# Sums of squares of four norms as one 512-column product of a split operand, and the key column sums moved behind the kv projection, in a two-layer decoder trunk

## The chip, the cores and the metric

The kernel runs on one core of a Trainium2 chip. Its time is the device time of one execution in microseconds (us); before the change the median of three runs is 1017.04 us (1016.98 to 1017.77). One more execution was recorded by the hardware profiler. The engines are named as in its page: PE is the matrix engine, PEld its weight loads, DVE the vector engine, ACT the scalar engine, POOL GpSimd, SP the engine that issues the weight DMAs.

## What is computed

The input x is 256 tokens by 1024 numbers in float32. Two layers follow each other. Each is a macaron block: half a feed-forward, a mixer, half a feed-forward, each of them behind an RMS norm. The first mixer is a retention with 4 heads, the second a sliding-window attention with 16 query heads, whose keys and values are made once, from x as it stands after the first layer. Cut to what matters here:

```python
def rms_norm(x, g):
    y = x * rsqrt(mean(x * x, axis=-1) + 1e-6)
    return y * g

def swiglu(h, w_in, w_out):                    # 1024 -> 2 x 2816 -> 1024
    gate, up = split(h @ w_in, 2)
    return (silu(gate) * up) @ w_out

x = x + 0.5 * swiglu(rms_norm(x, g1), ...)     # feed-forward f = 0, norm m = 0
x = x + retention(rms_norm(x, gm))             #                     norm m = 1
x = x + 0.5 * swiglu(rms_norm(x, g2), ...)     # f = 1, m = 2
k, v = split(rms_norm(x, g_kv) @ w_kv, 2)      # the shared keys and values, of the same x as m = 3
k = rope(rms_norm(k))
x = x + 0.5 * swiglu(rms_norm(x, g1), ...)     # f = 2, m = 3
x = x + attention(rms_norm(x, gm), k, v)       #        m = 4
x = x + 0.5 * swiglu(rms_norm(x, g2), ...)     # f = 3, m = 5
```

## The kernel before

**Layout.** x lies transposed: 8 tiles of 128 features by 256 tokens. Each of the engines has its own program, written out by hand and tied to the others by semaphores (`wait_ge`, `then_inc`); nothing is scheduled by a tool. What stands first in an engine's program runs first, and a wait holds back all that stands behind it on that engine.

**Split products.** Every weight and every activation is held as two parts, high and low (`w_hi`, `w_lo`; `h` holds the high part of a tile in its first 256 columns and the low part in the next 256). A block of weights is used in a pair of products: `w_hi` with all 512 columns, then `w_lo` with the first 256. `weight_block` issues such pairs alternately; where `high_product` and `low_product` are called in loops, several high products come first and then as many low ones ("in passes").

**Weights.** They come in units of 2048 or 1408 columns through 4 slots. SP issues a unit's DMA once the slot is free, ACT makes `w_hi` (its `split`), DVE makes `w_lo = stage - w_hi` (its `split`, L648, counted by the semaphore `lo_ready`), and PE waits for `lo_ready` (or for `hi_ready` where it runs in passes).

**Norms.** The norm's factor is not applied to h but to the products. In a feed-forward's first groups of products (`in_group`, 8 blocks kt of 4 pairs each per group), PE also adds up the squares (`norm_sum`): a product of a 128 x 128 matrix of ones with `sq_sum`, both in plain float32, gives the sum in all rows of a PSUM bank. DVE reads it (`token_sums`, L668) and makes the inverse root (`token_scale`, nine small steps). For m = 2 and 3 `norm_sum` stands behind kt = 5 of group 0; for m = 0 and 5 behind kt = 4 of group 1. `sq_sum` is made on POOL tile by tile as x becomes ready (`square_sum`, L1122 to L1131), and for m = 0 on DVE (`first_sums`, L1073), in front of the split of weight unit 3.

**Key columns.** The keys are needed with tokens in rows, so their norm factor is needed as a column. For m = 3 `norm_sum` therefore also issues two products with 2 columns each (`ones` moving, `sq_sum` as weights), and DVE makes `r_col` from them in `token_scale` and counts `r_ready`. That is long before they are used.

**The end of feed-forward 2.** Its output tiles 0 to 5 are made in pairs (`out_tile`). Then PE runs the kv projection (`shared_kv`), and output tiles 6 and 7 in passes (`out_tile_in_passes`, L1295), whose weights are four units of their own (`last_out`). Meanwhile ACT waits for `r_ready`, copies keys and values out of PSUM with the factor, and DVE runs `shared_k` (L830), the norm and rotation of the keys; the DVE split of the last of the four units stands behind it, then the evacuation of tile 6 and two splits of the query weights, the evacuation of tile 7, one more split, and the rotation of the first queries (`q_rope`). PE then runs the query products and waits for that rotation before it transposes the queries (`q_transposes`, L1473).

## Time and profile before

| | |
|---|---|
| median of three runs | 1017.04 us (1016.98 to 1017.77) |
| the profiled execution | 1017.42 us, of which its span 1015.6 us |
| granted TensorE clock | 1.00 |
| PE busy | 1011.0 us, 100% |
| PE weight loads | 885.8 us, 87% |
| DVE busy | 780.5 us, 77% |
| ACT busy | 496.9 us, 49% |
| POOL busy | 95.9 us, 9% |

The span runs from the first to the last instruction; the 1.8 us around it belong to the execution as a whole. A busy PE is not a PE at its peak, since its instructions overlap: what one product costs is the distance from its start to the start of the next.

### The profile page before, as it was taken

How to read it: one execution, taken by the hardware profiler on the slowest of the kernel's cores; microseconds unless marked ns; L12 is line 12 of the kernel's file. 1: busy time of each engine (PE TensorE's matmuls, PEld its weight loads, DVE VectorE, ACT ScalarE, POOL GpSimd, SP SyncE). 2: the span in 40 equal slices, each digit the busy share in tenths (PEclk: the TensorE clock that was granted, in tenths of full speed). 3: DMA queues.
4: the chain of work that ended last, by engine and by line, in shares of the span. 5: the costliest groups of instructions: out<-in, count | busy, mean ns of one | idle time of the engine just before them, and what ended most of it. 6: DMA issues, size and time to landing. Idle time of an engine off the chain costs nothing.

```text
span 1015.6 us, 15838 instructions
## 1 busy us (share of the span) xinstructions
PE 1011.0 (100%) x5922; PEld 885.8 (87%) x5922; DVE 780.5 (77%) x874; ACT 496.9 (49%) x536; POOL 95.9 (9%) x91
## 2 busy tenths in 40 slices
PE   9999999999999999999999999999999999999998
PEld 8888888888888888888888888888897898888888
DVE  7988866787797787777767787787778977877743
ACT  7455435544443364454444454465447944554432
POOL 0000013101100151000013100000220041000000
PEclk9999999999999999999999999999999999999999
DMA  9664456652553454554455645545563345544461
GB/s 347 242 235 178 142 175 220 245 195 104 218 191 103 187 184 162 199 200 169 150 187 197 249 165 192 190 145 171 183 241 120 106 161 192 207 168 165 156 192 65
DMA packets 32295, 185.31 MB, mean 182 GB/s; under 512 B 3840, under 2 KB 6400, under 8 KB 16128
## 3 DMA queue, kind: packets, MB, share of 16 engines
q1 hardware_dynamic: 31968, 184.64, 50.8%
q8 instruction: 23, 0.38, 0.1%
q14 instruction: 16, 0.13, 0.1%
q10 hardware_dynamic: 288, 0.16, 0.1%
HBM read 183.73 MB, written 1.05 MB: 182 GB/s over the span
## 4 chain that ended last, share of the span: by engine, by line
PE 100%; issue 0%; DVE 0%; DVEq 0%
PE ps L1159 99%; PE ps L1506 1%; PE ps L1473 0%; PE ps L1465 0%; DVE x L813 0%; DVE ones L1086 0%; DVEq L1085 0%; DVEq L1084 0%; DVEq L1083 0%; DVEq L1082 0%; DVEq L1081 0%
## 5 line engine op out<-in xcount | busy, mean ns | idle before, releaser
L1159 PE MATMUL ps<-h,w_hi 128*128 128x512 f32 x1664 | 563.3, 394 | 0.0
L1159 PE MATMUL ps<-h,w_lo 128*128 128x256 f32 x1664 | 437.8, 278 | 0.0
L648 DVE TENSOR_TENSOR w_lo<-stage,w_hi 128x2048 fp32r<-128x2048 f32 (+1 forms) x190 | 397.2, 2100 | 32.5 <-ACT w_hi L333 32.3
L1159 PEld LDWEIGHTS ps<-h,w_hi 128*128 128x128 f32 x1664 | 310.0, 188 | 68.5 <-issue 0.3
L333 ACT ACTIVATE w_hi<-stage 128x2048 fp32r<-128x2048 f32 (+1 forms) x190 | 326.9, 1728 | 6.4 <-PE ps L1159 6.2
L1159 PEld LDWEIGHTS ps<-h,w_lo 128*128 128x128 f32 x1664 | 304.8, 188 | 3.3
L1159 PE MATMUL ps<-act_t,w_hi 128*128 128x512 f32 (+1 forms) x726 | 240.0, 386 | 0.0
L1159 PE MATMUL ps<-act_t,w_lo 128*128 128x256 f32 x704 | 189.3, 278 | 0.0
L1159 PEld LDWEIGHTS ps<-act_t,w_hi 128*128 128x128 f32 x726 | 134.4, 188 | 29.0
L365 ACT ACTIVATE tmp<-ps 128x1024 f32<-128x1024 f32 x44 | 45.1, 1025 | 193.4 <-PE ps L1159 193.4
L1159 PEld LDWEIGHTS ps<-act_t,w_lo 128*128 128x128 f32 x704 | 130.0, 188 | 0.3
L712 DVE TENSOR_TENSOR tmp<-ps,tmp 128x1024 f32<-128x1024 f32 x44 | 53.8, 1224 | 70.0 <-ACT tmp L365 70.0
L398 ACT ACTIVATE tmp<-ps 128x256 f32<-128x256 f32 x39 | 14.9, 381 | 119.1 <-PE ps L1159 119.1
L1159 PE MATMUL ps<-w_hi,h 128*128 128x512 f32 x192 | 60.3, 395 | 0.0
L758 DVE SCALAR_TENSOR_TENSOR tmp<-ps,tmp 128x256 f32<-128x256 f32 x39 | 16.5, 422 | 54.0 <-ACT tmp L398 54.0
L370 ACT ACTIVATE tmp<-tmp 128x512 f32<-128x512 f32 x44 | 27.9, 633 | 58.9 <-DVE tmp L718 58.9
L718 DVE TENSOR_TENSOR tmp<-tmp,r_row 128x1024 f32<-128x1024 f32 x44 | 53.9, 1225 | 1.5
L1131 POOL TENSOR_TENSOR sq_sum<-sq_sum,sq 128x256 f32<-128x256 f32 x35 | 48.5, 1384 | 2.8
L1122 POOL TENSOR_TENSOR sq_sum<-x 128x256 f32<-128x256 f32 x5 | 3.1, 614 | 442.8 <-DVE x L760 379.7
L1128 POOL TENSOR_TENSOR sq<-x 128x256 f32 x35 | 31.0, 885 | 130.6 <-DVE x L760 128.6
L1159 PEld LDWEIGHTS ps<-w_hi,h 128*128 128x128 f32 x192 | 35.1, 188 | 7.8 <-issue 0.7
L687 DVE SCALAR_TENSOR_TENSOR h<-x,gain,h 128x256 fp32r<-128x256 f32 (+1 forms) x48 | 32.7, 682 | 10.2 <-ACT h L344 10.1
(158 smaller groups left out, 711.0 us busy)
## 6 DMA issues: line engine op xcount, KB each, us to landing
stage<-w_in_dram SPq DMA_DIRECT2D x85, 1024.0 KB, 4.8
stage<-w_out_dram SPq DMA_DIRECT2D x64, 704.0 KB, 4.0
stage<-w_ret_dram SPq DMA_DIRECT2D x24, 1024.0 KB, 4.9
stage<-w_ret_out_dram SPq DMA_DIRECT2D x8, 1024.0 KB, 4.8
stage<-w_q_dram SPq DMA_DIRECT2D x4, 1024.0 KB, 6.2
stage<-w_o_dram SPq DMA_DIRECT2D x4, 1024.0 KB, 4.8
stage<-w_in_dram SPq DMA_DIRECT2D x8, 256.0 KB, 4.3
stage<-w_in_dram SPq DMA_DIRECT2D x2, 512.0 KB, 6.3
```

The source lines that it names most:

```text
L333: nc.scalar.activation(w_hi[:, s, 0:n], stage[:, s, 0:n], ACT.Copy).then_inc(hi_ready, 1)
L365: nc.scalar.activation(t, ps[:, 4 * (g % 2):4 * (g % 2) + 4, T:2 * T], ACT.Copy).then_inc(in_lo_half, 1)
L370: nc.scalar.activation(tmp[:, g % 2, 0:512], tmp[:, g % 2, 0:512], ACT.Silu).then_inc(in_silu, 1)
L398: nc.scalar.activation(tmp[:, d % 2, 0:T], ps[:, bank, T:2 * T], ACT.Copy, scale=scale).then_inc(out_lo_half, 1)
L648: nc.vector.tensor_tensor(w_lo[:, s, 0:n], stage[:, s, 0:n], w_hi[:, s, 0:n].bitcast(F32), ALU.subtract).then_inc(lo_ready, 1)
L687: nc.vector.scalar_tensor_tensor(h[:, ds(d + per * i, 1), T:2 * T], x[:, ds(d + per * i, 1), :], gain[:, ds(m * DT + d + per * i, 1)], h[: ...
L712: nc.vector.tensor_tensor(t, ps[:, 4 * (g % 2):4 * (g % 2) + 4, 0:T], t, ALU.add).then_inc(in_free, 1)
L718: nc.vector.tensor_tensor(t, t, same(r_row[:], 4), ALU.mult).then_inc(in_scaled, 1)
L758: chain.step(nc.vector.scalar_tensor_tensor(t, ps[:, bank, 0:T], scale, t, ALU.mult, ALU.add))
L1128: nc.gpsimd.tensor_tensor(sq[:].rearrange("p (a n) -> p a n", a=1), x[:, ds(i + 1, 1), :], x[:, ds(i + 1, 1), :], ALU.mult).then_inc(sq_do ...
L1131: nc.gpsimd.tensor_tensor(sq_sum[:], sq_sum[:], sq[:], ALU.add).then_inc(sum_added, 1)
L1159: return nc.tensor.matmul(out_, w, x_, start=start, stop=stop)
```

## The change

Three things change. For the four norms ahead of feed-forwards (m = 0, 2, 3, 5) the sum of squares is itself split into a high and a low part, side by side in `sq_parts`, and `norm_sum` is one product of 512 columns in the type of the split weights; DVE adds the two halves with a second instruction. The block of four pairs in front of that product is issued alternately instead of in passes. And the two key column products move from `norm_sum` (m = 3) to behind the kv projection, with the DVE steps for `r_col` in front of `shared_k`; tiles 6 and 7 of feed-forward 2 are made with `out_tile`, so alternately.

```diff
                 dve.wait_ge(sum_done, sums_before(m) + 1)
-                ins = nc.vector.tensor_scalar(n_v[:], ps[:, FIRST_SUM if m in LATE_NORMS else SUM, 0:T], V_SCALE / D, V_SCALE * EPS,
-                                              ALU.mult, ALU.add)
-                if m == 3:
-                    ins = nc.vector.tensor_scalar(col_v[:], ps[:, SUM, T:T + 4], V_SCALE / D, V_SCALE * EPS, ALU.mult, ALU.add)
+                bank = FIRST_SUM if m in LATE_NORMS else SUM
+                ins = nc.vector.tensor_scalar(n_v[:], ps[:, bank, 0:T], V_SCALE / D, V_SCALE * EPS, ALU.mult, ALU.add)
+                if m in FFN_NORM:
+                    ins.then_inc(half_added, 1)
+                    dve.wait_ge(half_added, FFN_NORM.index(m) + 1)
+                    ins = nc.vector.scalar_tensor_tensor(n_v[:], ps[:, bank, T:2 * T], V_SCALE / D, n_v[:], ALU.mult,
+                                                         ALU.add)
                 ins.then_inc(sum_read, 1)
...
                 rsqrt(n_v[:], n_t[:], r_row[:])
-                if m == 3:
-                    rsqrt(col_v[:], col_t[:], r_col[:])
-                    nc.vector.tensor_copy(col_t[:], r_col[:]).then_inc(r_ready, 1)
+
+            def key_columns():
+
+                dve.wait_ge(columns_done, 1)
+                chain.step(nc.vector.tensor_scalar(col_v[:], ps[:, COLUMNS, T:T + 4], V_SCALE / D, V_SCALE * EPS,
+                                                   ALU.mult, ALU.add))
+                rsqrt(col_v[:], col_t[:], r_col[:])
+                nc.vector.tensor_copy(col_t[:], r_col[:]).then_inc(r_ready, 1)
...
                     out_evac(m, 5, (u + 14, u + 15), 0.5)
+                    key_columns()
                     shared_k()
                     split(FIRST["kv", 0] + 4)
...
-                nc.vector.tensor_tensor(sq_sum[:], x_sq[:, 0, :], x_sq[:, 1, :], ALU.add).then_inc(sum_added, DT)
+                nc.vector.tensor_tensor(sq_all[:], x_sq[:, 0, :], x_sq[:, 1, :], ALU.add).then_inc(sum_added, DT)
+                dve.wait_ge(sum_added, DT)
+                nc.vector.tensor_scalar(sq_parts[:, 0:T], sq_all[:], 1.0, None, ALU.mult).then_inc(sq_hi, 1)
+                dve.wait_ge(sq_hi, 1)
+                nc.vector.tensor_tensor(sq_parts[:, T:2 * T], sq_all[:], sq_parts[:, 0:T].bitcast(F32),
+                                        ALU.subtract).then_inc(sq_lo, 1)
...
+                if parts:
+                    pool.wait_ge(sum_added, added_for(m) - 1)
+                    pool.wait_ge(x_done, CREDIT + DT * m)
+                    nc.gpsimd.tensor_tensor(sq[:], x[:, DT - 1, :], x[:, DT - 1, :], ALU.mult).then_inc(sq_done, 1)
+                    pool.wait_ge(sq_done, (DT - 1) * m)
+                    nc.gpsimd.tensor_tensor(sq_all[:], sq_sum[:], sq[:], ALU.add).then_inc(sum_added, 1)
+                    n = FFN_NORM.index(m)
+                    pool.wait_ge(sum_added, added_for(m))
+                    nc.gpsimd.tensor_copy(sq_parts[:, 0:T], sq_all[:]).then_inc(sq_hi, 1)
+                    pool.wait_ge(sq_hi, n + 1)
+                    nc.gpsimd.tensor_tensor(sq_parts[:, T:2 * T], sq_all[:], sq_parts[:, 0:T].bitcast(F32),
+                                            ALU.subtract).then_inc(sq_lo, 1)
...
                 pe.wait_ge(sum_added, added_for(m))
-                if m in (3, ATT):
-                    for t in range(2):
-                        last = matmul(ps[:, SUM, T + 2 * t:T + 2 * t + 2], sq_sum[:, t * P:(t + 1) * P],
-                                      ones[:, 0:2], True, True)
-                if m != ATT:
-                    last = matmul(ps[:, FIRST_SUM if m in LATE_NORMS else SUM, 0:T], ones[:], sq_sum[:], True, True)
+                if m == ATT:
+                    last = column_sums(SUM, sq_sum)
+                elif m in FFN_NORM:
+                    pe.wait_ge(sq_lo, FFN_NORM.index(m) + 1)
+                    last = matmul(ps[:, FIRST_SUM if m in LATE_NORMS else SUM, :], ones[:].bitcast(F32R), sq_parts[:],
+                                  True, True)
+                else:
+                    last = matmul(ps[:, SUM, 0:T], ones[:], sq_sum[:], True, True)
                 last.then_inc(sum_done, 1)
...
-                        ahead_of_sum = g == 0 or (g == 1 and kt <= 4) if m in LATE_NORMS else m == 2 and kt <= 5
+                        ahead_of_sum = g == 0 or (g == 1 and kt <= 3) if m in LATE_NORMS else m == 2 and kt <= 4
...
                 if f == 2:
                     shared_kv()
+                    column_sums(COLUMNS, sq_all).then_inc(columns_done, 1)
                     for d in range(2):
-                        out_tile_in_passes(f, d, pairs)
+                        out_tile(f, d, pairs)
```

Where instructions move, the programs of the engines show it. The first place is DVE's program at the very start, where the squares of the input are added up ahead of the split of weight unit 3. Before:

```order
L1077 TENSOR_TENSOR x_sq<-x_sq 128x1024
L1078 TENSOR_TENSOR x_sq<-x_sq 128x512
L1079 TENSOR_TENSOR sq_sum<-x_sq 128x256
L648 TENSOR_TENSOR w_lo<-stage,w_hi 128x2048
L712 TENSOR_TENSOR tmp<-ps,tmp 128x1024
```

The same place in the changed kernel:

```order
L1090 TENSOR_TENSOR x_sq<-x_sq 128x1024
L1091 TENSOR_TENSOR x_sq<-x_sq 128x512
L1092 TENSOR_TENSOR sq_all<-x_sq 128x256
L1094 TENSOR_SCALAR sq_parts<-sq_all 128x256
L1096 TENSOR_TENSOR sq_parts<-sq_all,sq_parts 128x256
L652 TENSOR_TENSOR w_lo<-stage,w_hi 128x2048
L724 TENSOR_TENSOR tmp<-ps,tmp 128x1024
```

Two instructions of 256 columns now stand in front of the split.

The second place is DVE's program behind the kv projection; `w_lo` of 1408 columns is the split of the third `last_out` unit, `k_a` begins `shared_k`. Before:

```order
L687 SCALAR_TENSOR_TENSOR h<-x,gain,h 128x256
L648 TENSOR_TENSOR w_lo<-stage,w_hi 128x1408
L836 TENSOR_TENSOR k_a<-kv_nat 128x256
L837 TENSOR_REDUCE hs_110<-k_a 128x4
L838 TENSOR_SCALAR hs_111<-hs_110 128x4
```

The same place in the changed kernel:

```order
L690 TENSOR_SCALAR col_v<-ps 128x4
L657 TENSOR_SCALAR r_col<-col_v 128x4
L663 TENSOR_TENSOR col_t<-r_col 128x4
L664 TENSOR_TENSOR col_t<-col_t,col_v 128x4
L665 SCALAR_TENSOR_TENSOR col_t<-col_t 128x4
L666 SCALAR_TENSOR_TENSOR r_col<-col_t,r_col 128x4
L661 SCALAR_TENSOR_TENSOR col_t<-r_col 128x4
L664 TENSOR_TENSOR col_t<-col_t,col_v 128x4
L665 SCALAR_TENSOR_TENSOR col_t<-col_t 128x4
L666 SCALAR_TENSOR_TENSOR r_col<-col_t,r_col 128x4
L693 COPY col_t<-r_col 128x4
L849 TENSOR_TENSOR k_a<-kv_nat 128x256
```

Eleven small instructions of 4 columns each, which stood behind the inverse root of m = 3, now stand between the split and `shared_k`.

The third place is POOL's program at the end of each `square_sum` ahead of a feed-forward. Before, the loop is followed by the next use of the routine:

```order
L1128 TENSOR_TENSOR sq<-x 128x256
L1130 REGISTER_ALU
L1131 TENSOR_TENSOR sq_sum<-sq_sum,sq 128x256
L1123 REGISTER_ALU
L1123 COMPARE_AND_BRANCH
L1122 TENSOR_TENSOR sq_sum<-x 128x256
```

In the changed kernel:

```order
L1150 TENSOR_TENSOR sq_sum<-sq_sum,sq 128x256
L1142 REGISTER_ALU
L1142 COMPARE_AND_BRANCH
L1154 TENSOR_TENSOR sq<-x 128x256
L1156 TENSOR_TENSOR sq_all<-sq_sum,sq 128x256
L1159 CAST sq_parts<-sq_all 128x256
L1161 TENSOR_TENSOR sq_parts<-sq_all,sq_parts 128x256
L1140 TENSOR_TENSOR sq_sum<-x 128x256
```

The last tile's square and addition are written out, and a copy and a subtraction follow them.

## Rows read from the trace of the kernel before

**Rows 1.** Page, part 1: busy time, share of the span and instructions of each engine

```profile
PE 1011.0 (100%) x5922; PEld 885.8 (87%) x5922; DVE 780.5 (77%) x874; ACT 496.9 (49%) x536; POOL 95.9 (9%) x91
```

**Rows 2.** Timeline of PE around the sum of m = 0: start, duration, engine, instruction

```profile
23.13 1.09 PE L1159 MATMUL ps<-h,w_hi 128*128 128x512 f32 x4
24.06 0.64 PE L1159 MATMUL ps<-h,w_lo 128*128 128x256 f32 x4
24.54 0.60 PE L1159 MATMUL ps<-sq_sum,ones 128*128 128x256 f32 x2
...
25.31 0.40 PE L1159 MATMUL ps<-h,w_hi 128*128 128x512 f32 x1
...
40.22 0.39 PE L1159 MATMUL ps<-h,w_hi 128*128 128x512 f32 x1
```

**Rows 3.** Timeline of PE around the sum and the key columns of m = 3

```profile
577.35 0.50 PE L1159 MATMUL ps<-ones,sq_sum 128*128 128x2 f32 x4
...
578.58 0.39 PE L1159 MATMUL ps<-h,w_hi 128*128 128x512 f32 x1
```

**Rows 4.** Timeline of DVE, then of the weight loads, in the first 30 us

```profile
20.25 0.43 DVE L1079 TENSOR_TENSOR sq_sum<-x_sq 128x256 f32<-128x256 f32 x1
20.59 2.28 DVE L648 TENSOR_TENSOR w_lo<-stage,w_hi 128x2048 fp32r<-128x2048 f32 x1
...
28.66 0.29 DVE L653 TENSOR_SCALAR r_row<-n_v 128x256 int32<-128x256 int32 x1
...
23.02 0.77 PEld L1159 LDWEIGHTS ps<-h,w_hi 128*128 128x128 f32 x4
```

**Rows 5.** Timeline of DVE: first and last of the ten steps of `r_col`

```profile
582.96 0.17 DVE L653 TENSOR_SCALAR r_col<-col_v 128x4 int32<-128x4 int32 x1
...
584.74 0.17 DVE L681 COPY col_t<-r_col 128x4 f32<-128x4 f32 x1
```

**Rows 6.** Timeline of ACT, then of DVE, from the kv projection to the queries

```profile
743.65 0.62 ACT L440 ACTIVATE kv_nat<-ps,r_col 128x128 f32<-128x128 f32 x2 [2.43 <-PE ps L1159]
...
744.31 0.42 DVE L836 TENSOR_TENSOR k_a<-kv_nat 128x256 f32<-128x256 f32 x1 [0.40 <-ACT kv_nat L440]
...
750.12 1.62 DVE L648 TENSOR_TENSOR w_lo<-stage,w_hi 128x1408 fp32r<-128x1408 f32 x1
...
755.00 4.49 DVE L648 TENSOR_TENSOR w_lo<-stage,w_hi 128x2048 fp32r<-128x2048 f32 x2 [1.29 <-ACT w_hi L333]
...
766.35 0.69 DVE L825 TENSOR_TENSOR q_a<-q_a,q_b 128x512 f32<-128x512 f32 x1
...
777.81 0.69 DVE L825 TENSOR_TENSOR q_a<-q_a,q_b 128x512 f32<-128x512 f32 x1
```

**Rows 7.** Timeline of PE, then of the weight loads, from the kv projection on

```profile
743.45 2.68 PE L1159 MATMUL ps<-act_t,w_hi 128*128 128x512 f32 x11
...
758.78 0.60 PE L1465 MATMUL ps<-ident,k_twice 128*128 128x128 f32 x4
...
767.66 0.60 PE L1473 MATMUL ps<-ident,q_a 128*128 128x128 f32 x4
...
778.62 0.42 PEld L1473 LDWEIGHTS ps<-ident,q_a 128*128 128x128 f32 x4 [0.21 <-issue]
```

**Rows 8.** Timelines of DVE, POOL and the weight loads, end of the retention

```profile
364.09 2.29 DVE L648 TENSOR_TENSOR w_lo<-stage,w_hi 128x2048 fp32r<-128x2048 f32 x1 [0.79 <-ACT w_hi L333]
...
364.19 2.79 POOL L1131 TENSOR_TENSOR sq_sum<-sq_sum,sq 128x256 f32<-128x256 f32 x1
...
389.06 0.61 POOL L1128 TENSOR_TENSOR sq<-x 128x256 f32 x1 [3.97 <-DVE x L760]
389.75 0.81 POOL L1131 TENSOR_TENSOR sq_sum<-sq_sum,sq 128x256 f32<-128x256 f32 x1
...
391.25 2.29 DVE L648 TENSOR_TENSOR w_lo<-stage,w_hi 128x2048 fp32r<-128x2048 f32 x1 [1.29 <-ACT w_hi L333]
...
393.76 0.31 PEld L1159 LDWEIGHTS ps<-sq_sum,ones 128*128 128x128 f32 x2
```

More of the change, by code:

```diff
@@ L195, in trunk @@
     ps = nc.alloc_psum_tensor("ps", [P, 8, 512], F32)
-    SUM, FIRST_SUM = 7, 3
+    SUM, FIRST_SUM, COLUMNS = 7, 3, 3
     sem = nc.alloc_semaphore
@@ L1122, in square_sum @@
                 nc.gpsimd.tensor_tensor(sq_sum[:], x[:, 0, :], x[:, 0, :], ALU.mult).then_inc(sum_added, 1)
-                with pool.Fori(0, DT - 1) as i:
+                parts = m in FFN_NORM
+                with pool.Fori(0, DT - 2 if parts else DT - 1) as i:
                     pool.wait_ge(sum_added, added_for(m) - DT + 1 + i)
@@ L1293, in ffn @@
                     out_tile(f, 1, pairs, whole_block)
[L1295 to L1308 removed]
             def out_tile(f, d, i, block=weight_block):
                 m, u0 = FFN_NORM[f], FIRST["out", f]
+                if f == 2 and isinstance(i, int):
+                    u0 = FIRST["last_out", f] - 4 * i
                 pe.wait_ge(x_done, DT * m + d + 1 + 2 * i)
```

22 lines of the change are left out of this document (9 added, 13 removed).

## The prediction, made before the changed kernel ran

> **What bounds the kernel now.** I read the page's busy times first: PE is busy 1011.0 of 1015.6 us [rows 1], DVE 780.5. So nearly every microsecond that PE's stream gets longer or shorter is one of the total, and work on DVE, ACT or POOL costs nothing until PE waits for it. Then I read PE's timeline around each place that the change touches, by the distances between starts, and last, for each of these places, how long before PE's need the other engines are done. The reader is to see in those rows what a sum costs PE, and how little air there is at two places.
>
> **PE's own work, removed and added.** A pair of products in alternation takes 0.347 us (14.91 us from 25.31 to 40.22 for 43 pairs), in passes 0.353 (23.13 to 24.54, four pairs) [rows 2]. The float32 sum of 256 columns starts at 24.54 and the second pair behind it at 25.31: 0.77 for one pair and the sum, so the sum costs 0.42. The new sum is one product of 512 columns of the split type. Four such, the high ones of a pass, start 0.93 apart in all, 0.23 each [rows 2]; I take 0.23, so 0.19 is saved at each of m = 0, 2 and 5, together 0.57. Should the new product cost as much as the old, that is nothing; it can't cost less than 0.23, since no wide product in the rows does.
>
> At m = 3 the key columns and the sum together take 577.35 to 578.58, 1.23 less one pair of 0.35, so 0.88 [rows 3]. With the new sum 0.23 stays, and 0.65 goes. Of that 0.88 less 0.42, so 0.46, are the key columns, which come back behind the kv projection. The blocks in front of the three other sums gain 0.006 a pair, 0.02 each, 0.07 for all three with rounding. PE's stream therefore loses 0.57 + 0.65 + 0.07 = 1.29 us before the kv projection, and there it gains 0.46 and loses at most 44 x 0.006 = 0.26 by the alternation of tiles 6 and 7 (0.1 if a long pass costs less per pair than a short one). What counts there is decided by a wait, below.
>
> **The start: two steps ahead of a split that was just in time.** DVE's split of unit 3 runs 20.59 to 22.87, and PE starts to load weights from it at 23.02 [rows 4]. That is 0.15 us of air, and a semaphore from DVE to PE takes about 0.12 (the rotation ends at 778.50 [rows 6], PE's load starts at 778.62 [rows 7]), so 0.03 is left. The change puts two dependent steps in between: a copy of 256 columns, 0.29 as the one-input step of the same size, and a subtraction, 0.43 as the addition ahead of it [rows 4], with some 0.03 of gap before each. The split moves by 0.78 and PE waits 0.75 (0.6 to 0.9 with other gaps; nothing only if the two steps ran beside the split, which one engine can't do). Behind PE's wait stands its whole program, and nothing later in the first feed-forward hands it back. I take 0.75.
>
> **Behind the kv projection: the key columns go from covered to exposed.** Before, ACT takes the keys out of PSUM at 743.65, as soon as PE is done, because `r_ready` was counted long ago; DVE's `k_a` follows at 744.31 [rows 6]. Now PE first issues the columns: they would start where tile 6 did, at 743.45 [rows 7], and are done 0.50 later [rows 3], 743.95. DVE reads them (0.2 with the gap) and does the ten steps from 582.96 to 584.91, 1.95 us [rows 5]: `r_ready` comes at about 746.13, ACT's copies start at 746.17 in place of 743.65, and everything behind them on DVE is 2.5 us late.
>
> Who waits for that? First the split of the fourth `last_out` unit: it ended at 751.74 [rows 6], now 754.26. PE needs it after three half tiles, 743.45 + 0.46 + 3 x 3.83 = 755.4 (a half tile is a quarter of 743.45 to 758.78 [rows 7]): 1.1 us of air, so the switch from `hi_ready` to `lo_ready` is free. Next the two splits of the query weights: they start at 755.00 and follow on tile 6's evacuation through ACT, so they start at 757.5, the first ends near 759.8, and PE wants it at about 759.5: a wait of 0.4. Then tile 7's evacuation, one more split, and the rotation of the first queries, whose last step ended at 767.04 [rows 6] with PE's transposes at 767.66 [rows 7]: it now ends at 769.6, and PE waits there again. On the way DVE was busy or waited for ACT, and ACT waited for DVE's x; these 1.29 us idles [rows 6] are part of the chain and absorb nothing. At last the second rotation, 778.50 then, 781.0 now; there PE's load engine already sat idle 0.21 us before the change [rows 7], so no air is left at all and PE is late by the full 2.5. From there both engines go on 2.5 us later. This is not beside the 0.46 and the 0.1 to 0.26 above but contains them: PE reaches the waits 0.4 later or 0.1 earlier and stands there until DVE is done. I take 2.5; the ends are 0.2 (all of DVE's lateness absorbed, only the columns left: 0.46 less 0.26) and 3.5 (the small steps at 0.3 in place of 0.2 us each).
>
> **POOL's two more steps.** At m = 2 POOL's last addition ends at 390.56 and PE loads the sum's weights at 393.76 [rows 8]. A copy and a subtraction come in between. The subtraction is an addition of 0.81. The trace shows no copy on POOL; its nearest row is the square of one tile, 0.61, an upper bound, and the lower is nothing. Taken alone they are done by 392.1, 1.6 us early. But DVE's split starts at 391.25, and the trace shows what that can do: the addition at 364.19 came 0.10 behind the start of a split (364.09 to 366.38) and took 2.79 in place of 0.81, so it ran only once the split was over [rows 8]. If the subtraction starts before 391.25 the split is the one to wait, and it has time. If it starts after, it ends at 393.54 + 0.7 = 394.2, PE's load goes to 394.3, and that costs 0.5. The copy must take less than about 0.5 us. A one-input step should be cheaper than one that reads two operands, so I take no collision: 0, with 0.5 as the other end.
> The Trainium skill, "SBUF — State Buffer", section "SBUF: two separate sides", calls the port pair that DVE and GpSimd share an exclusive lock: whoever starts first has it for the whole instruction, and the other is blocked. The row at 364.19 agrees, and by this rule the order of two starts some tenths apart decides over 0.5 us here. By "GPSIMD Engine Reference" of the Trainium skill, section "Elementwise — side-by-side cycle accounting", a loop body of at most two operations takes 1.03 cycles an element and a two-input step about 2.6, which at 1.2 GHz makes the copy an estimated 0.22 us plus dispatch; no row of before shows it, and by that figure the subtraction would win the race.
> At m = 3 and 5 the same two steps follow a tile that ends as far ahead of its sum or further, and I take them as hidden, collision or not. DVE's added instruction in `token_sums` (0.43, as the addition of rows 4) delays the root by half a microsecond, while PE has 8 pairs or more, 2.8 us, until it waits for the read; hidden.
>
> **The sum.** -1.29 + 0.75 + 2.5 = +1.96 us. It is made on the profiled execution, 1017.42 us (span 1015.6 and 1.8 around it), which gives 1019.4. That execution was 0.4 above the median, so for the median I say 1017.04 + 1.96 = 1019.0 us. What a measurement of this kernel can tell from no change is 0.2%, 2.03 us; the forecast lies on that line, 1019.07, just inside it.
>
> **Rivals.**
> - A, the race on the shared port is lost: as above plus 0.5, 1019.5. For it: POOL's steps have gaps of about 0.1 and the margin is 0.2 or less. Against: the copy reads one operand.
> - B, DVE catches up before the first transposes, so it is not slower: the place is the stretch from the kv projection to 767.66, the price falls from 2.5 to 0.2. It decides whether the rotation that ended at 767.04 moves by less than PE's 0.62 of air. Then -1.29 + 0.75 + 0.2 = -0.3: 1016.7, no change. Against: no idle of DVE there is free of its own chain.
> - C, as B, and the first split is not late for PE either: -1.29 + 0.2 = -1.1, 1015.9. It needs both waits to be absent; rows 4 speak against it.
> - D, the late chain grows: if the small steps take 0.3, or PE's restarts behind its waits each cost some tenths, the 2.5 becomes 3.5 and the whole 1020.0; with the race lost too, 1020.5.
> - E, the new sum is no cheaper than the old one (the low half, or the switch to it, eats the gain): 4 x 0.19 dearer, 1019.8.
>
> **Chances and range.** Forecast 0.42, A 0.18, B 0.15, C 0.06, D 0.12, E 0.07. A, D and E lie above 1019.07, 0.37 together, and 0.15 of the forecast's 0.42 does too: slower 0.52. No change has the other 0.27 of the forecast and B and C but for 0.03, so 0.45; faster has that 0.03. No case reaches 1015.0, where faster begins, without a gain that no row shows. The forecast's own range is 1018.5 to 1019.5. The range that should hold 8 in 10 takes in A, most of D and E, and most of B: 1016.6 to 1020.4.
>
> **What would show it.** In the changed profile: PE's distance from the 512-column sum's start to the next start near 0.23; PE idle about 0.75 us near 23, with the weight load behind it at 23.8 in place of 23.02; `kv_nat` 2.5 us after the kv projection's end; PE idle before the query products and before the first two transposes of queries, in all a span from the kv projection's end to the second transposes 2.5 us longer than the 35.2 of before. At the end of the retention, the copy on POOL under 0.5 us and the subtraction 0.8, not 2.8. The forecast is wrong if PE shows no wait at 23 us, if the first transposes follow at the old distance, or if the sum takes PE 0.4 us or more.

## The result, and the profile after

The changed kernel takes a median of 1022.17 us in 15 executions (1018.75 to 1022.47), the kernel before 1017.31 in 15 (1016.98 to 1017.83): a ratio of 1.0034 by the means (1.0048 by the medians), 95% interval 1.0027 to 1.0042. The prediction was 1019.0, its range 1016.6 to 1020.4. But the 15 times are not spread, they lie in two groups: 7 at 1018.75 to 1019.50 and 8 at 1022.17 to 1022.47, with nothing between them. The kernel before has one group. The granted clock is 1.00 in both groups (0.999 in single executions), so it is not the clock that parts them. The profiled execution is of the lower group (1019.50 us, span 1017.7), and there the prediction's steps can be read one by one.

The page of the kernel after (against [rows 1]):

```profile
span 1017.7 us, 15830 instructions
PE 1010.2 (99%) x5918; PEld 888.0 (87%) x5918; DVE 783.3 (77%) x880; ACT 497.0 (49%) x536; POOL 99.2 (10%) x97
```

PE is busy 0.8 us less than before in a span 2.1 us longer: in this execution PE waits more, it does not work more.

The start, from the timelines of DVE, the weight loads and PE (answering [rows 4] and [rows 2]; in brackets the idle time of the engine before the row and what ended it):

```profile
20.92 0.29 DVE L1094 TENSOR_SCALAR sq_parts<-sq_all 128x256 fp32r<-128x256 f32 x1
21.24 0.43 DVE L1096 TENSOR_TENSOR sq_parts<-sq_all,sq_parts 128x256 fp32r<-128x256 f32 x1
21.59 2.28 DVE L652 TENSOR_TENSOR w_lo<-stage,w_hi 128x2048 fp32r<-128x2048 f32 x1
...
23.92 0.19 PEld L1190 LDWEIGHTS ps<-h,w_hi 128*128 128x128 f32 x1 [1.49 <-DVE w_lo L652]
...
25.44 0.40 PE L1190 MATMUL ps<-sq_parts,ones 128*128 128x512 f32 x1
25.68 0.40 PE L1190 MATMUL ps<-h,w_hi 128*128 128x512 f32 x1
```

The two steps stand in front of the split, PE waits for it, and the new product costs 25.44 to 25.68, 0.24, as worked out. The sum starts 0.90 later than before (24.54 in [rows 2]).

The kv projection and what follows, from the timelines of PE, ACT, DVE and the weight loads (answering [rows 6, 7]):

```profile
743.29 0.50 PE L1190 MATMUL ps<-ones,sq_all 128*128 128x2 f32 x4
...
746.07 0.63 ACT L444 ACTIVATE kv_nat<-ps,r_col 128x128 f32<-128x128 f32 x2 [5.01 <-DVE col_t L693]
...
746.73 0.43 DVE L849 TENSOR_TENSOR k_a<-kv_nat 128x256 f32<-128x256 f32 x1 [0.75 <-ACT kv_nat L444]
...
759.68 0.30 PEld L1190 LDWEIGHTS ps<-w_hi,h 128*128 128x128 f32 x2 [0.33 <-DVE w_lo L652]
...
769.34 0.42 PEld L1501 LDWEIGHTS ps<-ident,q_a 128*128 128x128 f32 x4 [1.39 <-DVE q_a L838]
...
780.73 0.42 PEld L1501 LDWEIGHTS ps<-ident,q_a 128*128 128x128 f32 x4 [0.59 <-issue]
```

PE waits at the three places that the prediction named: 0.33 before the query products, 1.39 before the first transposes, and 0.59 in place of 0.21 before the second. From the kv projection's end to the second transposes 37.44 us pass (743.29 to 780.73), 35.17 before (743.45 to 778.62).

The race on the shared port at m = 2, from the timelines of POOL, DVE and the weight loads (answering [rows 8]):

```profile
391.29 0.40 POOL L1159 CAST sq_parts<-sq_all 128x256 fp32r<-128x256 f32 x1
391.77 0.74 POOL L1161 TENSOR_TENSOR sq_parts<-sq_all,sq_parts 128x256 fp32r<-128x256 f32 x1
...
391.94 2.72 DVE L652 TENSOR_TENSOR w_lo<-stage,w_hi 128x2048 fp32r<-128x2048 f32 x1 [1.32 <-ACT w_hi L337]
...
394.45 0.19 PEld L1190 LDWEIGHTS ps<-sq_parts,ones 128*128 128x128 f32 x1
```

POOL's subtraction starts 0.17 us ahead of the split and takes its 0.74; the split is the one that is held (2.72 in place of 2.29). The race is won, narrowly.

Nothing in this profile holds the other 3.2 us. For that a profile of the upper group is needed. The changed kernel itself was never profiled in it, but the first set of experiments brought one of a near relative, and what it showed is best told here: e3 below (the split sums without the moved key columns) was profiled in its upper group (1020.79 us). The view of windows gives PE's busy time and the count of its products, here of e3, under it of the changed kernel and last of the kernel before:

```profile
40.00:180.00 140.00, 140.00 (x794) 1.00 0.52 183
400.00:560.00 160.00, 160.00 (x925) 1.00 0.52 181
```

```profile
40.00:180.00 140.00, 140.00 (x810) 1.00 0.53 187
400.00:560.00 160.00, 160.00 (x925) 1.00 0.51 178
600.00:720.00 120.00, 120.00 (x694) 1.00 0.51 176
```

```profile
40.00:180.00 140.00, 140.00 (x810) 1.00 0.53 183
```

PE is busy without a gap in all three, at the same granted clock of 1.00, yet in the first feed-forward e3 gets through 794 products in place of 810. (All five profiles of an upper group, of e3, e6, e7, e10 and e13, count 794 or 795 in that window; the other fifteen 808 to 810.) The timeline shows how, first e3, then e1 (the changed kernel again), each from one pair's high product to that of the eleventh pair behind it:

```profile
59.89 0.40 PE L1190 MATMUL ps<-h,w_hi 128*128 128x512 f32 x1
...
63.78 0.40 PE L1190 MATMUL ps<-h,w_hi 128*128 128x512 f32 x1
```

```profile
59.79 0.39 PE L1190 MATMUL ps<-h,w_hi 128*128 128x512 f32 x1
...
63.60 0.39 PE L1190 MATMUL ps<-h,w_hi 128*128 128x512 f32 x1
```

Eleven pairs take 3.89 us in one and 3.81 in the other: 353.3 against 346.7 ns a pair, as the mean over 20 us of either gives it more closely. So the same stream of the same products has two rhythms. The slow one holds from the sum of m = 0 (25.6) to the retention (199), some 490 pairs, and 490 x 6.6 ns are 3.2 us: the distance between the groups.

### The profile page after: what moved, and what is told of

It reads as the page before. It is cut to its first block, busy times and chain, and to the rows that moved or that the text cites. A ratio compares the mean times of both kernels' runs of the same rounds, so it can differ in the third digit from the quotient of the medians.

```text
span 1017.7 us, 15830 instructions
## 1 busy us (share of the span) xinstructions
PE 1010.2 (99%) x5918; PEld 888.0 (87%) x5918; DVE 783.3 (77%) x880; ACT 497.0 (49%) x536; POOL 99.2 (10%) x97
## 4 chain that ended last, share of the span: by engine, by line
PE 93%; DVE 3%; ACT 1%; DMA 1%; SPq 1%; issue 1%; DVEq 0%; ACTq 0%
PE ps L1190 93%; DVE w_lo L652 1%; DMA stage<-w_in_dram 1%; ACT w_hi L337 1%; ACT s_two L530 0%; DVE sm L1005 0%; SPq L293 0%; SPq L291 0%; PE ps L1534 0%; DVE hs L892 0%; ACT x_sq L625 0%; DVE q_a L838 0%; DVE q_a L832 0%; DVE q_b L835 0%; DVE x_sq L1090 0%
## 5 line engine op out<-in xcount | busy, mean ns | idle before, releaser
L1190 PE MATMUL ps<-act_t,w_hi 128*128 128x512 f32 (+1 forms) x726 | 244.6, 385 | 0.0
L1190 PE MATMUL ps<-act_t,w_lo 128*128 128x256 f32 x704 | 197.2, 280 | 0.0
L1190 PEld LDWEIGHTS ps<-act_t,w_lo 128*128 128x128 f32 x704 | 133.1, 189 | 0.0
L1150 POOL TENSOR_TENSOR sq_sum<-sq_sum,sq 128x256 f32<-128x256 f32 x32 | 46.1, 1440 | 2.5
```

The source lines that it names most:

```text
L1150: nc.gpsimd.tensor_tensor(sq_sum[:], sq_sum[:], sq[:], ALU.add).then_inc(sum_added, 1)
L1190: return nc.tensor.matmul(out_, w, x_, start=start, stop=stop)
```

## The experiments

Each set was run together with the kernel before on one chip, and the five sets (e1 to e4, e5 to e8, e9 to e12, e13 to e15, e16 to e18) on five chips; the median of the kernel before stayed at 1017.3 to 1017.5. "Upper group" means executions some 3.2 us above the others of the same kernel.

**e1: the changed kernel again.**

> The changed kernel, unchanged. Its 15 times fall in two groups, 7 at 1018.75 to 1019.5 us and 8 at 1022.2 to 1022.5, those of the kernel before in one (1017.0 to 1017.8). The profiled execution is of the lower group (1019.5, span 1017.7). All theories expect both groups again; what counts is a profile of the upper one, 3.1 us longer. Theory P (port): at the end of a sum of squares POOL's subtraction has to start ahead of a DVE split; in the lower group it did by 0.17 us at m = 2 (391.77 against 391.94) and by 0.19 at m = 3 (573.26 against 573.45). Where it loses, POOL shows a copy or a subtraction of 2.5 to 3 us (0.40 and 0.74 otherwise) and PE a wait before the product of 512 columns; from the rows 0.6 us at m = 2 and up to 1.0 at m = 3, so P must show another wait behind to reach 3.1. Theory K (kv): the chain behind the key columns, late by 2.5 us, sometimes misses something more; PE then shows its added wait between 743 and 830. Theory S (start): DVE's later split of unit 3 delays the loads that follow it, and PE shows the added wait before 60 us.

1018.70, 1019.26, 1022.42, 1022.47 and 1023.41: two groups again. The profile, wanted of the upper one, fell in the lower one (span 1016.8), with a wait at the start of 0.29 where the first had 1.49: the start varies by 0.9 us from one execution to the next, the rest does not. From the sum's start to the span's end it is the same to 0.02 in both (992.26 and 992.28, read to the nanosecond). This stretch, which leaves the start out, compares two profiles far better than their times do.

**e2: the key columns alone.**

```
-  all split sums (copy, subtraction, 512 columns, second read)
+  matmul(..., ones, sq_all if m == 3 else sq_sum)   # float32, as before
   column_sums(COLUMNS, sq_all) behind shared_kv(), out_tile() there
```

> All four sums as float32 products of 256 columns as before, nothing added on DVE at the start or on POOL; only the key columns are behind the kv projection and the two tiles there alternate. By the prediction's steps: 0.46 less at m = 3, 2.5 more behind the kv projection, about +2.0 against before: 1019.3. Theory K: a second group 3.1 us above that in about half of the executions, as the changed kernel. Theories P and S: one group only. If the chain's price were not what the prediction says but the rest of the change, this kernel would be within 0.3 of before.

1019.50 (1019.08 to 1019.82, 11 executions), one group; ratio 1.0021, interval 1.0012 to 1.0030. The step's +2.0 is measured as +2.1, and K is out: the second group does not come from the kv projection.

**e3: the split sums alone.**

```
-  column_sums(COLUMNS, sq_all) behind shared_kv(); out_tile()
+  if m == 3: column_sums(6, sq_all)   # ahead of the sum; out_tile_in_passes()
```

> The four sums as one split product with their steps on DVE and POOL, as in the changed kernel; the key columns are taken again at m = 3 ahead of the sum (out of the float32 sum of squares, in a bank of their own), and the two tiles behind the kv projection go in passes as before. By the prediction's steps: 4 x 0.19 and 0.07 less, 0.75 to 0.9 more at the start: 0.1 less to 0.1 more than before, 1017.2 to 1017.4 in a lower group. Theories P and S: a second group some 3 us above it. Theory K: one group only.

Six executions at 1017.03 to 1017.75 and five at 1020.10 to 1020.87. The lower group is at 1017.3, as expected; the upper one belongs to the split sums. Theory P (the shared port) is out as well: the profile is of the upper group, and POOL's subtractions took 0.74 and 0.75 in it at m = 2, 3 and 5.

**e4: the start's two steps behind the split.**

```
-  first_sums() [copy, subtract inside]; split(3)
+  first_sums(); split(3); copy; subtract
```

> The changed kernel with DVE's copy and subtraction of m = 0 moved from ahead of the split of unit 3 to behind it; PE's sum at about 24.5 us needs them by then, and they end near 23.8. By the prediction's step at the start the wait of 0.75 (0.9 in the profile) goes: the lower group at 1018.2 to 1018.4 in place of 1019.1, with PE's first load from the split of unit 3 at 23.0. Theory S: one group only. Theories P and K: the second group stays, 3.1 above. If the wait at the start came from something else, the time stays at 1019.1.

1018.94 and 1019.21, and 1021.77, 1021.95 and 1022.11. S in its simple form is out: the profile, of the lower group, shows PE without a wait at the start, and the second group is still there. The gain of 0.75 did not show in the lower group (two executions) and is about 0.4 in the upper; with so few and a start that varies, this doesn't price the step. e14 does.

**e5: m = 0 in float32.**

```
-  matmul(ps[:, 3, :], ones, sq_parts)        # m = 0
+  matmul(ps[:, 3, 0:T], ones, sq_sum)        # m = 0, and no copy or subtraction
```

> The changed kernel with the sum of m = 0 alone as a float32 product of 256 columns again, straight from DVE's last addition (no copy, no subtraction). In the profile of the upper group the alternating pairs of the whole first feed-forward, 25.6 to 199 us, follow at 353.3 ns, in every profile of a lower group at 346.7; 491 pairs by 6.6 ns are the 3.2 us. Theory R: PE's alternating stream can settle into either rhythm behind the sum of m = 0, and the float32 sum (0.42 us, two weight loads ahead of its products) lets it settle into the fast one always. It expects one group, at the lower one plus 0.19 for the sum and less 0.45 for the start: about 1018.9. Rival Q: the four alternating pairs ahead of the sum, which stay, bring the slow rhythm: two groups again.

1018.86 (1018.36 to 1019.23, 11 executions; 1.0015, interval 1.0006 to 1.0024), one group, where it was expected. Q is out.

**e6: the pairs ahead of the split sum of m = 0 in passes.**

```
-  ahead_of_sum = g == 0 or (g == 1 and kt <= 3)
+  ahead_of_sum = g == 0 or (g == 1 and kt <= 4)     # m = 0
```

> The changed kernel with the last four pairs ahead of the sum of m = 0 in passes (four high, four low products) again, as before; the sum is the split product. Rival Q expects one group at 1019.1. Theory R in its narrow form, that only the form of the sum counts, expects two groups, 3.1 us apart, in about the same shares. The four pairs themselves are worth 0.02 us.

Two of six at 1019.03 and 1019.19, four at 1022.02 to 1023.07. Alternation ahead of the sum is thus not needed for the slow rhythm.

**e7: a small float32 product behind the split sum. e9: a long one.**

```
   matmul(ps[:, 3, :], ones, sq_parts)
+  matmul(ps[:, 0, 0:2], sq_all[:, 0:P], ones[:, 0:2])     # e7
+  matmul(ps[:, 0, 0:T], ones, sq_all)                     # e9
```

> The changed kernel with one more product right behind the split sum of m = 0: float32, 2 columns, out of the float32 sum of squares into a bank that is free, its result unused. It costs about 0.23 us (half of the key columns' 0.46). Theory R in the form that any float32 product resets the rhythm expects one group at about 1019.3. If it is the length of the sum (0.42 us) and not its kind that gives the weight loads their lead, two groups stay, at 1019.3 and 1022.5. Rival Q: two groups.

> As e7, but the unused float32 product behind the split sum of m = 0 has 256 columns in place of 2, so it is the old sum itself, behind the new one: 0.42 us more than the changed kernel. With 2 columns all 5 executions were in the upper group, with the 256-column float32 sum alone none of 22 (e2, e5). Theory R (a long float32 product gives the weight loads their lead, and the fast rhythm follows whatever stood before): one group at about 1019.5. Rival T: any product with a length of its own only shifts the phase in which the pairs begin, and what follows is as it falls: an upper group at 1022.7 in part or all of the executions.

e7: all five at 1022.25 to 1022.67. e9: ten of eleven at 1019.31 to 1019.90, one at 1023.40. A float32 product as such is thus no cure (R in that form is out), and the long one makes the fast rhythm likely, not certain. That the small one makes the slow rhythm more frequent than in the changed kernel (11 of 20 in the first result and e1, on other chips) is not shown by five executions: at that share all five would be slow in one case of twenty.

**e8 and e16: what the findings point to.**

```
   e5, and:
-  column_sums(COLUMNS, sq_all) behind shared_kv()
+  if m == 3: column_sums(6, sq_all)                   # ahead of the sum
   e16 also: out_tile() -> out_tile_in_passes() behind the kv projection
```

> What the steps point to: the sum of m = 0 as float32 product as before, the sums of m = 2, 3 and 5 as split products, the key columns at m = 3 as before (in a bank of their own), the two tiles behind the kv projection in alternation. By the prediction's steps: 3 x 0.19 = 0.57 less, 0.05 for the blocks, and up to 0.26 for the alternation of the tiles, nothing at the start and no late chain: 0.6 to 0.9 less than before, 1016.4 to 1016.8, and by theory R one group. If the late chain behind the kv projection were due to the alternation rather than to the key columns, the gain would be gone: 1017.5 or more.

> As e8, but the two tiles behind the kv projection in passes as before. In e8 they alternated, and ran at 353.3 ns a pair (743.1 to 758.3 us), so the alternation gained nothing there, and the second query transposes came 35.6 us behind the last kv product, 35.4 before. What is left against before: 0.57 for the sums of m = 2, 3 and 5, and 0.05 for blocks, 1016.7 to 1016.8, one group. If e8's tiles cost nothing, the time is e8's 1017.0.

e8: 1016.97 (1016.61 to 1017.24) against 1017.29. e16: 1016.93 (1016.35 to 1017.29) against 1017.46, ratio 0.9994, interval 0.9985 to 1.0003. Both are one group of 11 with a median 0.3 and 0.5 us below before. The interval of each ratio still reaches past 1 (e8: 0.9991, 0.9978 to 1.0003), so the time alone does not prove the gain; e16's profile has a span of 1014.6 with the sum at

```profile
24.07 0.59 PE L1186 MATMUL ps<-sq_sum,ones 128*128 128x256 f32 x2
```

so 990.5 us from there to the end, and 991.1 before (1015.6 less 24.54 in [rows 2]): 0.6 less of the part that does not vary, where the expectation had 0.57 and 0.05 together. In e8 the alternating tiles ran in the slow rhythm, on their timeline

```profile
743.10 0.40 PE L1186 MATMUL ps<-act_t,w_hi 128*128 128x512 f32 x1
...
758.29 0.40 PE L1186 MATMUL ps<-act_t,w_hi 128*128 128x512 f32 x1
```

43 pairs in 15.19 us, 353.3 each. In the changed kernel the same tiles had run at 346.7. From the sum to the end e8 has 990.8, 0.3 more than e16: the alternation lost there.

**e10: the split sum of m = 0 as two products.**

```
-  matmul(ps[:, 3, :], ones, sq_parts)
+  matmul(ps[:, 3, 0:T], ones, sq_parts[:, 0:T]); matmul(ps[:, 3, T:2*T], ones, sq_parts[:, T:2*T])
```

> The changed kernel with the split sum of m = 0 as two products of 256 columns, the high half and then the low half, in place of one of 512. They take about 0.12 each, so the length is the same to 0.01 us; only the pattern of the stream changes. Theory R: the pattern ahead of the pairs is a short one as before, two groups, 1019.1 and 1022.3. Rival T: the phase is another, so the shares change: one group, upper or lower.

1019.06, and 1021.83 to 1023.02 four times: two groups, as R forecast; T had forecast one. With five executions neither is settled by it.

**e11: the race at m = 2 lost.**

```
+  if m == 2: gpsimd.tensor_copy(sq, sq_all)      # once more, on e5
   gpsimd.tensor_copy(sq_parts[:, 0:T], sq_all); subtract
```

> As e5 (m = 0 in float32, one group at 1018.9, span 1017.0), with POOL's copy at m = 2 made twice, so that the subtraction comes 0.48 us later, behind the start of DVE's split (391.94 in the changed kernel, POOL's subtraction at 391.77). Rival A of the prediction: the subtraction is held until the split is over, ends near 394.9 and PE waits about 0.5 to 0.6 us before the product of 512 columns; POOL's subtraction shows 2.7 to 2.9 us in place of 0.74. If the two can run side by side it shows 0.74, ends at 393.0, and nothing waits.

1026.11 us, one execution, 7.3 above e5. From the timelines of POOL and the weight loads, and PE's windows:

```profile
391.72 2.66 POOL L1160 TENSOR_TENSOR sq_parts<-sq_all,sq_parts 128x256 fp32r<-128x256 f32 x1
...
394.50 0.19 PEld L1189 LDWEIGHTS ps<-sq_parts,ones 128*128 128x128 f32 x1 [0.61 <-issue]
```

```profile
400.00:560.00 160.00, 160.00 (x907) 1.00 0.50 176
600.00:720.00 120.00, 120.00 (x681) 1.00 0.48 170
```

The subtraction is held (2.66 in place of 0.74), and PE's weight load comes 0.61 late: rival A's mechanism and its own wait, as forecast. But behind that wait the second and the third feed-forward run in the slow rhythm (925 and 694 products in the same windows of the changed kernel). Rhythm and wait together are 7.1 us (some 990 pairs x 6.6 ns = 6.5, and 0.6), and from the sum of m = 0 to the end the two profiles differ by 7.05 (999.56 against e5's 992.51). The window by which the race is won in the changed kernel, 0.17 us, guards 7 us and not 0.5. It is one execution; e15 below repeats the slow rhythm in four.

**e12: the tiles behind the kv projection in passes, the key columns still there.**

```
-  out_tile(f, d, pairs)
+  out_tile_in_passes(f, d, pairs)      # on e5
```

> As e5, with the two tiles behind the kv projection in passes again, while the key columns stay behind it. By the prediction the chain of DVE behind the key columns decides and the tiles' products are covered by it: PE comes to its waits 0.26 us later and leaves them at the same time, 1018.9 as e5 and 37.6 us from the last kv product to the second query transposes in both. If instead the alternation of the tiles is what makes PE late, the span falls by up to 2 us, to 1016.9.

1018.61 (1018.28 to 1019.02) against e5's 1018.86. From the key columns to the second query transposes it has 742.76 to 780.22, 37.46, and e5 742.51 to 779.95, 37.44. So the form of the tiles is covered by DVE's chain, and it is the key columns with their DVE steps that cost the time.

**e13: only the sum of m = 0 split, nothing else.**

```
   kernel before, with at m = 0:
-  matmul(ps[:, 3, 0:T], ones, sq_sum)
+  matmul(ps[:, 3, :], ones, sq_parts)      # copy, subtraction behind split(3)
```

> The kernel before with one thing changed: the sum of m = 0 is the split product of 512 columns, its copy and subtraction behind DVE's split of unit 3, so that PE has no new wait; the pairs ahead of it are in passes as before, all other sums float32, the key columns at m = 3. Theory R (it is the form of the sum at m = 0): two groups, one 0.19 under before (1017.1), one 3.2 above that (1020.3). Rival W (it takes a wait of PE shortly before the sum, or the alternation ahead of it, to bring the slow rhythm): one group at 1017.1.

Five executions at 1020.34 to 1021.06 (a sixth, at 3410 us, is left out as disturbed); no lower group at all, where R had forecast two. The sum and the window in its profile:

```profile
24.30 0.40 PE L1172 MATMUL ps<-sq_parts,ones 128*128 128x512 f32 x1
24.54 0.40 PE L1172 MATMUL ps<-h,w_hi 128*128 128x512 f32 x1
```

```profile
40.00:180.00 140.00, 140.00 (x795) 1.00 0.52 184
```

From the sum's start to the end it has 994.14 us and the kernel before 991.09: 3.05 more, which is the 3.2 of the rhythm less the sum's own 0.2. One product in place of another, 0.2 us shorter by itself, makes the kernel 3 us slower, and PE has no new wait (DVE's two steps and its second read are new too, but nothing on PE waits for them). Rival W is out for m = 0.

**e14: only the start late, float32 sum.**

```
   kernel before, with:
+  copy; subtract      # ahead of split(3); PE waits for both, sum in float32
```

> The kernel before with only the lateness of the start: DVE makes the copy and the subtraction of m = 0 ahead of the split of unit 3 and PE waits for both, but the sum stays the float32 product, everything else as before. It prices the start alone. The prediction's step says 0.75 more than before, 1018.0; the profiles so far, in which the start varies from one execution to the next by more than that, say 0.3 to 0.6: 1017.6 to 1017.9. Theory R: one group. Rival W: a second group 3.2 above.

1017.93 (1017.60 to 1018.58, 11 executions) against 1017.36 (1.0007, interval 0.9998 to 1.0016): 0.57 for the start (the interval reaches down to nothing), one group, though PE waited 0.98 in the profile just eight products ahead of the sum. From the sum to the end its profile has 991.09, exactly as before.

**e15 and e18: the lost race with a float32 sum, and with the wait earlier.**

```
   e11, with at m = 2:
-  matmul(ps[:, 7, :], ones, sq_parts)
+  matmul(ps[:, 7, 0:T], ones, sq_all)      # behind the same wait
   e18 also: wait_ge(sq_lo, 1) four pairs earlier
```

> As e11, where the lost race made PE wait before the sum of m = 2 and the second and third feed-forward, 394.8 to 744 us, ran at 353.3 ns a pair (988 pairs by 6.6 are 6.5 us): the same late parts on POOL and the same wait of PE for them, but the sum of m = 2 itself is the float32 product of 256 columns. Theory R: the fast rhythm, so the price of the lost race is only its wait of 0.6 and the float32 sum's 0.19 over e5: 1019.6. Rival W (the wait brings the slow rhythm, whatever the sum's form): 1026.3.

> As e15 (lost race at m = 2, float32 sum behind PE's wait of 0.6, slow rhythm from 394.8 to 744, 1026.2), but PE waits for POOL four alternating pairs ahead of the sum in place of right before it, so the wait grows by their 1.4 us to 2.0. At m = 0 a wait eight products ahead of a float32 sum left all 11 executions fast (e14). Theory V (only a wait that ends right at the sum leads into the slow rhythm): 1019.6 plus 1.4, 1021.0. Rival W (any wait shortly before the alternation at m = 2): 1027.6.

e15: 1025.73 to 1026.66, four of four. e18: 1020.77 to 1021.12 in four, one at 1024.07, though its wait is longer, and its windows are those of the fast rhythm. The waits on the weight loads, e15 then e18, and a window of each:

```profile
393.93 0.30 PEld L1189 LDWEIGHTS ps<-sq_all,ones 128*128 128x128 f32 x2 [0.61 <-issue]
```

```profile
394.14 0.19 PEld L1189 LDWEIGHTS ps<-h,w_hi 128*128 128x128 f32 x1 [1.87 <-issue]
```

```profile
400.00:560.00 160.00, 160.00 (x907) 1.00 0.51 177
```

```profile
400.00:560.00 160.00, 160.00 (x925) 1.00 0.51 177
```

So the float32 sum is no protection when PE waits right in front of it, and a wait three times as long, four pairs earlier, leaves the fast rhythm in the profile and, by the times, in four of five: theory V of e18's expectation holds there, with the one at 1024.07 open. This fells theory R as a rule.

**e17: passes behind the split sum.**

```
   e13, with:
-  ahead_of_sum: g == 1 and kt <= 4
+  ahead_of_sum: g == 1 and kt <= 5
```

> As e13 (before with the split sum at m = 0, all 5 executions in the upper group, 1020.3 to 1021.1), with the four pairs right behind the sum in passes too; the alternation begins four pairs later. Theory T (the phase in which the alternation begins decides, and the passes change it): the upper group is gone or seldom, 1017.2. If it is the split sum itself that leaves PE's loads without a lead, whatever four products follow: again all in the upper group, 1020.7.

One of six at 1017.54 (the profiled one, in the fast rhythm), five at 1020.36 to 1021.28: T's forecast, the upper group gone or seldom, missed.

**What the set says together.** At m = 0 the split sum without a long float32 product behind it had the upper time in 42 of 63 executions (8 of 15 of the changed kernel; then 3 of 5, 5 of 11, 3 of 5, 4 of 6, 5 of 5, 4 of 5, 5 of 5 and 5 of 6 in e1, e3, e4, e6, e7, e10, e13 and e17). The float32 sum in its place had it in none of 65 (e2, e5, e8, e12, e14, e16), and the contrast stands within each set, so on each chip. (e11, e15 and e18 have the float32 sum at m = 0 too; their profiles are fast there, but their times can't tell, because m = 2 is changed as well.) At m = 2 both forms have it behind a wait that ends right at the sum, and the split form was fast without that wait in every profile. What is left is T in its loose form: the stream of alternating pairs keeps the rhythm in which it starts, and the few products or waits in front set that start. In its sharper form T missed e10 and e17, as R missed e13 and e15.

The traces narrow it. The slow rhythm is a round of three pairs, six distances of 241, 120, 236, 113, 233 and 117 ns. In the 20 profiles, 43 split sums of one product come right behind alternating pairs, without a wait or another added product beside them. Of these, 23 come in the fast rhythm, and it goes on. The other 20 come in the slow round. In 17 of them (two at m = 0, all 15 at m = 5) the sum stands behind the 233 and the 117, takes 241 itself, and the fast rhythm follows. In three (e3 at m = 0, e11 and e15 at m = 3) it stands at another place of the round, and the slow rhythm goes on. So it is at m = 0 between the two groups; first e3 (slow behind the sum), then the changed kernel (fast):

```profile
25.03 0.40 PE L1190 MATMUL ps<-h,w_hi 128*128 128x512 f32 x1
25.27 0.28 PE L1190 MATMUL ps<-h,w_lo 128*128 128x256 f32 x1
25.39 0.40 PE L1190 MATMUL ps<-sq_parts,ones 128*128 128x512 f32 x1
25.63 0.39 PE L1190 MATMUL ps<-h,w_hi 128*128 128x512 f32 x1
```

```profile
25.09 0.40 PE L1190 MATMUL ps<-h,w_hi 128*128 128x512 f32 x1
25.32 0.28 PE L1190 MATMUL ps<-h,w_lo 128*128 128x256 f32 x1
25.44 0.40 PE L1190 MATMUL ps<-sq_parts,ones 128*128 128x512 f32 x1
25.68 0.40 PE L1190 MATMUL ps<-h,w_hi 128*128 128x512 f32 x1
```

The last pair ahead of the sum takes 0.36 in the one and 0.35 in the other. In both, PE starts these pairs behind its wait for DVE, and comes out of it at one place of the round in e3 and at another in the changed kernel's two profiles; if that differs from one execution of a kernel to the next, it gives two groups. It is a pattern in the traces and not a test: no run moved the sum by one pair, and the cases with passes ahead of the sum (e6 and e13 slow, e17 fast in its profile) or another product beside it (e7 and e10 slow, e9 fast) lie outside it. What inside PE holds the rhythm no view shows, and which form will be fast can't be said from this ahead of a run; this stays open. Of the kernel before, one execution in the 23 beside e5 to e8 took 1024.59 us. It was not profiled.

## Why the prediction was right and wrong

Where the prediction's steps are read in the lower group:

| step | forecast | measured |
|---|---|---|
| start, two steps ahead of the split | +0.75 | +0.57 (e14); 0.29 to 1.49 of idle in single profiles |
| sum of m = 0 (part of the next row) | -0.19 | -0.18 (0.24 in place of 0.42) |
| from the sum of m = 0 to the kv projection's end (m = 0, 2, 3, blocks) | -1.10 | -1.06 (718.91 to 717.85) |
| key columns behind the kv projection, to the second transposes | +2.5 | +2.27 (35.17 to 37.44) |
| from there to the end (m = 5) | -0.19 | -0.04 (237.01 to 236.97) |
| POOL's two steps at m = 2 | 0 | 0, race won by 0.17 |

The rows add up to the forecast's +1.96; the prediction's text puts the gain of m = 5 among the 1.29 that come before the kv projection, but that sum stands behind it, so 1.10 is due there and 0.19 later. The profiled execution has +0.90 - 1.06 + 2.27 - 0.04 = +2.07, the difference of the spans (1015.63 and 1017.70). The forecast's 1019.0 and its own range of 1018.5 to 1019.5 are the lower group's 1019.1. Some of that closeness is luck: by the table the start and the chain were priced 0.4 too high together, and the gain of m = 5 0.15 too high the other way. The places of all waits were right, and so was the reason that the kv chain contains the small gains and losses beside it (e12). The term for the chain was 0.2 too high: `k_a` comes 2.58 late against the kv projection's end (746.73 - 743.29 against 744.31 - 743.45), the second transposes 2.27. On DVE, measured in each kernel from its kv projection's end, this lateness shrinks in three steps: 2.58 up to the last split, 2.48 behind it, 2.39 from the first rotation on, 2.26 at the second. The gain of m = 5 is there, 0.13 from that sum's start to the end (168.79 to 168.66), but 0.09 is lost between the second transposes and the sum (68.22 to 68.32); e2, with the moved columns and float32 sums, shows the same 68.32 there, and e16, with the columns as before, 68.23. So that loss goes with the moved columns.

The step that failed is the first of the working: "A pair of products in alternation takes 0.347 us". It was read from one stretch of one execution [rows 2] and then held for all, before and after. The new sum was priced by its own length, 0.23, and that was near the measured 0.24; its effect on the 490 pairs behind it was not on the list, nor was it among the rivals. It is worth 3.2 us, some seventeen times the 0.19 that the edit saves at that place, and e13 shows it alone. So the median, in the upper group by 8 executions of 15, was missed by 3.2 us and lies above the range's 1020.4. With one execution fewer in that group the median would have been the lower group's, so the forecast of the median failed by a close split of the times, and the missing mechanism is the real miss. The rows of the kernel before show one rhythm of the alternation and gave no plain warning of a second. (Its passes take 0.353 a pair in [rows 2], the slow rhythm's distance; whether that is more than chance no run shows.)

Rival A did not come about, but e11 forced it: its mechanism was right (the subtraction held 2.66, PE 0.6 late) and its price of 0.5 wrong by more than a factor of ten, for the same reason. Rivals B and C are refuted by the three waits, D by the chain's 2.27, E by the 0.24. The rule of the Trainium skill that whoever starts first on the shared pair has it for the whole instruction ("SBUF — State Buffer", section "SBUF: two separate sides") agrees with the traces on both sides: won by 0.17 us, DVE's split took 2.72 in place of 2.29; lost, POOL's subtraction took 2.66 in place of 0.74. The copy on POOL took 0.40, inside the 0.5 that the prediction allowed it, and above the 0.22 estimated there from "GPSIMD Engine Reference", which left the dispatch out.

## What to carry to other kernels

Where one engine's back-to-back stream is the whole time, measure its distance per repeated group in nanoseconds in every stage, before and after: 2% of rhythm over a stage outweighed here every instruction that was saved in front of it, and the busy share showed 100% in both. Times in two groups mean that one profile is half the picture: take more until both groups have one. A moved step is to be priced by the wait that it exposes and not by its own length on the busy engine (0.46 us of key columns on PE cost 2.3, because 1.95 us of DVE steps hang on them), and a race that is won by 0.2 us should be counted with what stands behind it.

## What the runs showed of the hardware that I had not expected

PE's alternating pairs (512 columns, then 256, each with its weight load) settle into 346.7 or 353.3 ns a pair, at the same granted clock of 1.00, and hold the one or the other through loops: 173 us in the first feed-forward, and in e11 and e15 from 394.8 to 744 us, there across the sum of m = 3 too. A split sum at one place of the slow round ended it in all 17 cases. The first distances behind the sum of e13 are 236, 116, 224, 118, 233, 117 ns; then 241, 120, 236, 113, 233, 117 repeats, three pairs in 1060 ns, where the fast rhythm of the changed kernel has 230 and 117 in each pair, three in 1040. One product exchanged for another (e13) turned the slow executions from none of 16, on the same chip, to five of five.
